# Decay levels of a recurrent mixer: VectorE multiplies only the halves that change, ScalarE copies the rest

## The reference: what is computed

```
f = lb + (1 - lb) * sigmoid(f_logit);  log_f = log(f);  k = 1 - f;  q = silu(q) * scale
b = cumsum(log_f) over the tokens
a[t, s] = sum_k q[t, k] * k[s, k] * exp(b[t, k] - b[s, k])     for s <= t
o = a @ v   (and a state that carries the same decay from chunk to chunk)
```

## Time and profile before

| | |
|---|---|
| median of three executions | 1296.33 us |
| the profiled execution | 1297.8 us, its span 1296.0 us |
| TensorE busy | 1253.4 us (97%) |
| VectorE busy | 993.6 us (77%) |
| ScalarE busy | 617.4 us (48%) |
| recurrent heads at work | from 157 to 386 us of the span |
| mean granted TensorE clock | 0.986 of full speed |

### The profile page before, as it was taken

How to read it: one execution, slowest core, us unless ns; L and a number is a source line. 1 busy time by engine, 2 the same in 40 slices (tenths; PEclk the granted TensorE clock), 3 DMA queues, 4 the chain that set the end, 5 groups by cost and what they waited for, 6 DMA issues and landing times.

```text
span 1296.0 us, 20738 instructions
## 1 busy us (share of the span) xinstructions
PE 1253.4 (97%) x7190; PEld 1105.4 (85%) x7190; DVE 993.6 (77%) x1290; ACT 617.4 (48%) x875; POOL 50.3 (4%) x98
## 2 busy tenths in 40 slices
PE   5899899999999999999999999999999999999997
PEld 5788899998988888888888888888888888888886
DVE  4788799999898889688888797879777766545454
ACT  3335455555556644555444444444444444434342
POOL 0000100031130000000000000000000000000000
PEclk9789899999999999999999999999999999999999
DMA  9999788888798899758777777776666676555553
GB/s 338 387 386 350 274 292 282 275 285 292 244 314 284 296 355 355 263 178 292 243 225 232 241 230 239 238 245 212 191 184 192 194 260 213 194 194 194 195 195 114
DMA packets 155988, 329.44 MB, mean 254 GB/s; under 512 B 11493, under 2 KB 20438, under 8 KB 155026
## 3 DMA queue, kind: packets, MB, share of 16 engines
q1 hardware_dynamic: 152352, 318.49, 74.0%
q0 software_dynamic: 3280, 9.66, 2.2%
q10 hardware_dynamic: 290, 0.44, 0.1%
HBM read 322.77 MB, written 4.19 MB: 252 GB/s over the span
## 4 chain that ended last, share of the span: by engine, by line
PE 86%; DVE 5%; DMA 4%; ACT 2%; issue 2%; SPq 0%; DVEq 0%; ACTq 0%
PE bank L1281 23%; PE bank L1289 12%; PE bank L1346 6%; PE bank L1344 6%; PE bank L1345 6%; PE bank L1026 5%; PE bank L1028 5%; PE bank L1027 5%; PE bank L1013 4%; PE bank L1015 4%; PE bank L1016 4%; DMA pc<-in_w_ada 3%; DVE acc_c L1440 2%; DVE wlo L1428 1%; ACT whi L680 1%
## 5 line engine op out<-in xcount | busy, mean ns | idle before, releaser
L680 ACT ACTIVATE whi<-wraw 128x1024 fp32r<-128x1024 f32 x408 | 425.1, 1059 | 577.5 <-PE bank L1289 229.4
L1428 DVE TENSOR_TENSOR wlo<-wraw,whi 128x1024 fp32r<-128x1024 f32 x404 | 491.4, 1222 | 243.9 <-ACT whi L680 242.6
L1281 PE MATMUL bank<-h,whi 128*128 128x512 f32 x1400 | 334.7, 391 | 1.2 <-DVE h L1694 0.8
L1281 PEld LDWEIGHTS bank<-h,whi 128*128 128x128 f32 x1400 | 257.1, 188 | 51.8 <-issue 1.2
L1289 PEld LDWEIGHTS bank<-h,wlo 128*128 128x128 f32 x1400 | 179.6, 191 | 6.9
L1289 PE MATMUL bank<-h,wlo 128*128 128x256 f32 x1400 | 181.7, 283 | 0.0
L1013 PE MATMUL bank<-h,whi 128*128 128x256 f32 x512 | 149.0, 291 | 4.4 <-DVE h L1453 4.4
L1015 PE MATMUL bank<-h,whi 128*128 128x256 f32 x512 | 146.1, 285 | 0.0
L1016 PE MATMUL bank<-h,wlo 128*128 128x256 f32 x512 | 146.0, 285 | 0.0
L1344 PE MATMUL bank<-whi,act_hi 128*128 128x512 f32 x336 | 130.9, 389 | 0.0
L1346 PE MATMUL bank<-whi,act_lo 128*128 128x512 f32 x336 | 130.7, 389 | 0.0
(11 more groups left out here) (247 smaller groups left out, 1323.9 us busy)
## 6 DMA issues: line engine op xcount, KB each, us to landing
wraw<-in_w_up SPq DMA_DIRECT2D x176, 512.0 KB, 3.8
araw<-in_w_ada SPq DMA_DIRECT2D x128, 512.0 KB, 5.3
wraw<-in_w_in SPq DMA_DIRECT2D x112, 512.0 KB, 4.9
wraw<-in_w_down SPq DMA_DIRECT2D x88, 512.0 KB, 4.1
pc<-in_w_ada SPq DMA_DIRECT2D x48, 512.0 KB, 11.5
wraw<-in_w_out SPq DMA_DIRECT2D x32, 512.0 KB, 6.6
pc<-in_w_ada SPq DMA_DIRECT2D x32, 256.0 KB, 7.0
x<-in_x SPq DMA_DIRECT2D x2, 1024.0 KB, 8.3
```

The lines of the kernel that those rows point to most:

```text
L680: act.activation(whi[:, slot], wraw[:, slot], ACT.Copy).then_inc(s_hi, 1)
L1281: pe.matmul(ps[bank0 + f], whi[:, (ph.unit0 + j) % RING, k, f * P:(f + 1) * P], h[:, kk].rearrange("p a t -> p (a t)"), start=(kk == 0), s ...
L1428: dve.tensor_tensor(wlo[:, slot], wraw[:, slot], whi[:, slot].bitcast(F32), ALU.subtract).then_inc(s_lo, 1)
```

## The change

Three things. The factors are no longer kept per head with 1.0 between them: ScalarE writes f in place into `proj` for four heads ahead of time (steps `DECAY_AT`: 22, 22, 23, 23 and 51 to 54), and VectorE forms the factors of all levels for four heads at once in `decay_tree` (six dependent products of 512, 256, ... 16 elements, at steps 24 and 56). A level is now one VectorE product over the 256 elements that change, and one ScalarE copy (`keep`) of the 256 that don't. And there is one level a step, s0 to s0+5, with the merged keys one step behind each; everything later moves one step: `scores_b` to s0+8, the second `collect` to s0+9, the small `amat` copies to s0+10, `hgrn_out` to s0+11, the squares to s0+12. `ATT_AT` and the steps of the attention part are as before.

```diff
+DECAY_AT = [HGRN_AT[0] - 2 + hd // 2 if hd < 4 else HGRN_AT[4] - 9 + hd for hd in range(HEADS)]
+TREE_AT = [HGRN_AT[0], HGRN_AT[4]]
...
-            gp.memset(tot[:], 1.0).then_inc(s_cst, 1)
...
+            def keep(hd, l):
+
+                if l == 0:
+                    act.wait_ge(s_ks, hd + 1)
+                    act.wait_ge(s_qs, hd + 1)
+                else:
+                    act.wait_ge(s_lv, (LEVELS - 2) * hd + l)
+                    act.wait_ge(s_kept, (LEVELS - 2) * hd + l)
+                act.activation(kept(l + 1, l), kept(l, l), ACT.Copy).then_inc(s_kept, 1)
...
-                    if s == s0 - 1:
+                    if s == DECAY_AT[hd]:
                         act.wait_ge(s_ev, ev(GROUP["hf", hd // 4]))
-                        if hd:
-                            act.wait_ge(s_lv, (LEVELS - 2) * (hd - 1) + 2)
-                        else:
-                            act.wait_ge(s_lb, 1)
-                        sig = proj[:, HF + hd, :]
-                        act.activation(decays(0), sig.rearrange("p (b n c) -> p b n c", b=TB, c=2), ACT.Identity,
+                        act.wait_ge(s_lb, 1)
+                        act.activation(proj[:, HF + hd, :], proj[:, HF + hd, :], ACT.Identity,
                                        bias=lb[:, hd:hd + 1], scale=one_lb[:, hd:hd + 1]).then_inc(s_tot, 1)
...
-                    elif s == s0 + 2:
-                        merge_keys(hd, range(2))
-                    elif s == s0 + 4:
-                        merge_keys(hd, range(2, LEVELS - 1))
-                    elif s == s0 + 9:
+                    if s0 <= s < s0 + LEVELS - 2:
+                        l = s - s0
+                        keep(hd, l)
+                        if l:
+                            merge_keys(hd, l - 1)
+                    elif s == s0 + LEVELS - 2:
+                        merge_keys(hd, LEVELS - 3)
+                        last_level(hd)
+                        merge_keys(hd, LEVELS - 2)
+                    elif s == s0 + 10:
...
-                    elif s == s0 + 11:
+                    elif s == s0 + 12:
...
-                    elif s == HGRN_AT[hd] + 7:
+                    elif s == HGRN_AT[hd] + 8:
                         scores_b(hd)
-                    elif s == HGRN_AT[hd] + 10:
+                    elif s == HGRN_AT[hd] + 11:
                         hgrn_out(hd)
...
+            def decay_tree(g):
+
+                dve.wait_ge(s_tot, 4 * g + 4)
+                if g:
+                    dve.wait_ge(s_last, 3 * 4 * g)
+                for l in range(LEVELS - 2):
+                    a = decays_of_group(l, g)
+                    st.do(dve.tensor_tensor(decays_of_group(l + 1, g), a[:, :, ::2], a[:, :, 1::2], ALU.mult))
+                    st.wait()
+
             def level(hd, l):
-                w, n = 1 << l, P >> l
-                if l < LEVELS - 2:
-                    first, second = (factors_by_block(l)[:, :, e:e + n:2].rearrange("p b (n c) -> p b n c", c=2) for e in (1, n))
...
+                w = 1 << l
+                if l:
+                    dve.wait_ge(s_lv, (LEVELS - 2) * hd + l)
+                    dve.wait_ge(s_kept, (LEVELS - 2) * hd + l)
+                else:
+                    dve.wait_ge(s_ks, hd + 1)
+                factor = decays(l, hd).rearrange("p (n c) -> p c n", c=2).unsqueeze(3).to_broadcast([P, 2, P // w, w])
+                dve.tensor_tensor(changed(l + 1, l), changed(l, l), factor, ALU.mult).then_inc(s_lv, 1)
...
-                    if s == HGRN_AT[hd] + 8:
+                    if s == HGRN_AT[hd] + 9:
                         collect(hd, 1)
...
-                    elif s in (HGRN_AT[hd] + 1, HGRN_AT[hd] + 2, HGRN_AT[hd] + 3):
-                        l = 2 * (s - HGRN_AT[hd])
-                        level(hd, l - 1)
-                        if l < LEVELS - 2:
-                            level(hd, l)
-                    elif s == HGRN_AT[hd] + 5:
+                    elif HGRN_AT[hd] < s < HGRN_AT[hd] + LEVELS - 2:
+                        level(hd, s - HGRN_AT[hd])
+                    if s == HGRN_AT[hd] + 5:
                         collect(hd, 0)
+                for g in range(2):
+                    if s == TREE_AT[g]:
+                        decay_tree(g)
```

More of the change, by code:

```diff
@@ L433, in ev, with decays_of_group, decays, changed @@
             return 2 * n + 2
[L435 to L451, removed]
+        first_of = [0, 0]
+        for l in range(1, LEVELS - 1):
+            first_of.append(first_of[-1] + 4 * TB * (P >> l))
+        def decays_of_group(l, g):
+            if l == 0:
+                return proj[:, HF + 4 * g:HF + 4 * g + 4, :]
+            return tot[:, first_of[l]:first_of[l + 1]].rearrange("p (e x) -> p e x", e=4)
+        def decays(l, hd):
+            return decays_of_group(l, hd // 4)[:, hd % 4, :]
+        def changed(level, of):
+            w = 1 << of
+            base = qk[:, level, 0, w:w + 1]
+            return bass.AP(base.tensor, base.offset, [list(base.ap[0]), [2 * P - w, 2], [2 * w, P // w], [1, w]])
+        def kept(level, of):
+            w = 1 << of
+            base = qk[:, level, 0, 0:1]
+            return bass.AP(base.tensor, base.offset, [list(base.ap[0]), [2 * P + w, 2], [2 * w, P // w], [1, w]])
         def q_of(level, b):
-            return qk[:, level, b, b]
+            return qk[:, level, 3 * b]
         def k_of(level, b):
-            return qk[:, level, b, 1 - b]
+            return qk[:, level, 2 - b]
         def of_both(level, first, second):
@@ L757, in last_level, with merge_keys @@
                     act.activation(new[:, b, 0:w], old[:, b, 0:w], ACT.Copy,
[L758 to L768, removed]
-                    else:
-                        act.activation(k0[:].rearrange("p (n c w) -> p n c w", c=2, w=1), of_both(0, k_of(0, 0), k_of(0, 1)),
-                                       ACT.Copy).then_inc(s_km, 1)
+                                   scale=decays(LEVELS - 2, hd)[:, 2 * b + 1:2 * b + 2]).then_inc(s_last, 1)
+            def merge_keys(hd, l):
+                if l == LEVELS - 2:
+                    act.wait_ge(s_last, 3 * hd + 1)
+                else:
+                    act.wait_ge(s_lv, (LEVELS - 2) * hd + l + 1)
+                    act.wait_ge(s_kept, (LEVELS - 2) * hd + l + 1)
+                if l:
+                    act.activation(second_halves(k_of(l, 0), l), second_halves(k_of(l, 1), l), ACT.Copy).then_inc(s_km, 1)
+                else:
+                    act.activation(k0[:].rearrange("p (n c w) -> p n c w", c=2, w=1), of_both(0, k_of(0, 0), k_of(0, 1)),
+                                   ACT.Copy).then_inc(s_km, 1)
             for s in range(LATER - AHEAD, UP0):
@@ L1515, in second_norm @@
                                              op0=ALU.add, op1=ALU.mult).then_inc(s_colr, 1)
-            def level(hd, l):
-                w, n = 1 << l, P >> l
-                if l < LEVELS - 2:
-                    first, second = (factors_by_block(l)[:, :, e:e + n:2].rearrange("p b (n c) -> p b n c", c=2) for e in (1, n))
[L1521 to L1529, removed]
-                    dve.wait_ge(s_lv, (LEVELS - 2) * hd + l + 1)
-                    st.wait()
+            def decay_tree(g):
[6 more added lines that the diff above has]
+                    st.wait()
+            def level(hd, l):
+                w = 1 << l
+                if l:
+                    dve.wait_ge(s_lv, (LEVELS - 2) * hd + l)
+                    dve.wait_ge(s_kept, (LEVELS - 2) * hd + l)
+                else:
+                    dve.wait_ge(s_ks, hd + 1)
+                factor = decays(l, hd).rearrange("p (n c) -> p c n", c=2).unsqueeze(3).to_broadcast([P, 2, P // w, w])
+                dve.tensor_tensor(changed(l + 1, l), changed(l, l), factor, ALU.mult).then_inc(s_lv, 1)
             def first_level(hd):
-                queries = qk[:, 0].rearrange("p b a (n c) -> p (b a) n c", c=2)[:, ::3]
                 dve.wait_ge(s_ev, ev(GROUP["hq", hd // 4]))
```

31 lines of the change are left out of this document (18 added, 13 removed).

## The result

The changed kernel takes 1303.05 us (median of six, 1300.72 to 1304.86) against 1297.08 us (six, 1295.85 to 1298.98): ratio 1.0045, 95% interval 1.0035 to 1.0055. It is slower by 6.0 us; I had forecast slower by 4.0. The median lies 0.15 us inside the upper bound of my range (1303.2) and above the band of the forecast alone (1299.2 to 1301.6).

A forecast was written before the change was run, and what follows sets the result against it. TensorE was taken as the bound, its pauses in time deciding. Terms 1.0 - 1.0 + 2.66 - 0.24 + 1.57 = +4.0 us on the median of 1296.33 gave 1300.3 us, range 1297.2 to 1303.2.

The forecast's parts named there:

- TensorE's order decides: While the recurrent heads run, only TensorE's pauses count; VectorE's saved work is idle time unless a pause goes with it.
- Term c: Behind unit 90, TensorE waits before attention head 2's scores for ScalarE's small copies, now in step 90: +2.66 us.
- Term d: Behind the new pause at unit 90 the granted clock falls to half: +1.57 us, between 0 and 3.
- the small pause: The pause before `hgrn_out(7)`, now behind unit 91, goes: -0.24 us.
- The rival that the clock holds: The clock stays full behind unit 90: +2.4 us, 1298.8 us in all; chance 0.22.
- The row behind the 1.80 us pause: Earlier profile, before `scores_a` of head 0: half clock and a unit of 4.45 instead of 2.88 us, costing 1.57 us.
- Term b: The pause at 332 us, before attention head 0's transposes, goes because VectorE's reciprocal comes earlier: -1.0 us.
- the rival of late hand-overs: ScalarE late at step s0+11, between `hgrn_out` and the next `scores_a`: 0.5 us for seven heads, 1303.8 us; chance 0.15.
- my signs of being wrong: A pause under 2 us before the third attention head, or pauses before `scores_a` of heads 1 to 7.
- Term a: `scores_a(0)` waits for the second merged key in ScalarE's step 26, which comes later: +1.0 us, between 0 and +2.0.
- the clock is lost before and after alike: 0: At `scores_a(0)` the clock falls in both kernels, so it adds 0 us.
- The tree: VectorE's factor products: 3.1 us if strided, level 1 then 0.2 us late for ScalarE; 2.2 us and in time if plain.

The follow-up runs named there:

- e6: Changed kernel with one more VectorE product of 256 elements in each of the 48 levels, into a tile nothing reads: 1303.73 us, ratio 1.0059 to the kernel before.
- e1: Changed kernel with attention heads 2 and 3 one unit later (scores behind units 91 and 92): 1298.46 us, ratio 1.0014 to the kernel before.
- e3: Changed kernel with the first scores of recurrent head 0 alone behind unit 28 instead of 27: 1297.56 us, ratio 1.0003 to the kernel before.
- e2: Kernel before with only attention head 2's scores moved, behind unit 89 instead of 90: 1304.07 us, ratio 1.0051 to the kernel before.
- e9: Changed kernel with eleven small products of ones ahead of the wait behind unit 90: 1304.50 us, ratio 1.0056 to the kernel before.
- e12: Changed kernel with the two sines and their table load in ScalarE's step 28 instead of 26: 1301.32 us, ratio 1.0028 to the kernel before.
- e8: Kernel before with the first scores of recurrent head 0 alone behind unit 28 instead of 27: 1296.12 us, ratio 0.9993 to the kernel before.
- e10: Kernel before with first scores of recurrent head 0 behind unit 28 and attention head 0 one step later: 1299.99 us, ratio 1.0018 to the kernel before.

## Why the prediction was right, and where it was not

- **That TensorE's order decides and VectorE's relief is worth next to nothing: right.** e6 puts the work back for about 1 us; e1 and e3 change no work at all and move the time by 4.0 and 4.9.
- **Term c, the new pause: right.** 2.66 forecast, 2.66 measured in the changed kernel and the same idle time (2.50) in e2 and, unmended, in e3.
- **Term d, the clock: right in size.** 1.57 forecast; 1.6 by unit 91 (4.54 against 2.96 in the kernel before and 2.94 in e9). c and d with the small pause are 4.0 in the forecast and 4.0 by e1. The rival that the clock holds is out. The row behind the 1.80 us pause was a lucky guide all the same: idle stretches of 1.80, 2.50 and 2.78 us were followed by half clock, those of 0.83, 1.21, 1.47 and 1.78 us were not. 1.78 and 1.80 fall on different sides, so how long a stretch must be isn't shown, nor that its length alone decides.
  The Trainium skill's page "TensorE: Matmul & The Clock Gate" (section "Why this matters for your kernels") warns only of longer gaps, and that is not borne out here.
- **Term b, the pause at 332 us: wrong, 0 instead of -1.0.** The pause of the earlier trace rows did go, but one of the same length came at `hgrn_out(5)`, one unit earlier. The step that failed is "it can normalize by 330" with nothing late in its place: I followed VectorE's gain to the softmax, but not the softmax into ScalarE's step 73, where the table load and the exponentials take 2.2 us (325.46 to 327.65) and make the small copies late, which the change has just moved to step 74. I had put that price in the rival of late hand-overs (0.5 us for each of seven heads); it was one head and 1.0 us. So one of my signs of being wrong, a pause ahead of `scores_a` of a later head, was there once.
- **Term a, the first scores: right in kind, too small.** 1.0 forecast; +2.3 and +3.0 measured, like with like. Two steps of it failed. The first is ScalarE's start of step 24, "some 0.2 us later": the writes of f take 0.50 us each from start to start, not 0.3, so that four of them less the old one are 1.0 us. ScalarE in the changed kernel (first fence) and in e2 (second):

```profile
160.13 1.09 ACT L810 ACTIVATE proj<-proj,small 128x256 f32<-128x256 f32 x2
161.12 1.05 ACT L690 ACTIVATE whi<-wraw 128x1024 fp32r<-128x1024 f32 x1
...
169.03 0.25 ACT L789 ACTIVATE qk<-qk 128x64 f32<-128x64 f32 x1
```
```profile
160.10 1.10 ACT L680 ACTIVATE whi<-wraw 128x1024 fp32r<-128x1024 f32 x1
...
167.53 0.25 ACT L768 ACTIVATE qk<-qk 128x64 f32<-128x64 f32 x1
```

  From there to the second merged key it is 7.91 us, within 0.1 of what I had worked out. The scores start 1.5 us later between the late profiles (169.38 against 167.88) and 1.9 between the early ones (mean 167.7 against 165.77). The second step that failed is "the clock is lost before and after alike: 0". It holds between the early profiles. But in e2, which is the kernel before at this place, TensorE reached it 3.1 us later than in the kernel before's profile, idled 0.83 us, and the clock stayed at 1.00 behind it:

```profile
167.88 0.68 PE L1042 MATMUL bank<-proj,qk 128*128 128x128 f32 x4 [0.83 <-issue]
```
```profile
170.00:172.00 2.00, 2.00 (x20) 2.00 (x19) 1.97 (x4) 0.00 (x0) 0.00 (x0) 1.00 0.87 238
```

  Unit 28 took 2.96 us there, against 4.45 in the changed kernel: 1.5 us more. The changed kernel lost the clock at this place in seven profiles of seven that have it unmended, early or late.
- **The tree: cheaper than I took it.** 128 elements over every second value took 0.292 us, not the 0.401 of the earlier trace rows. It stays a near second at the first scores all the same (e12).
  The Trainium skill's page "SBUF — State Buffer" (section "Door 1: The DMA port swizzle", its note on cachelines) puts no penalty on a stride of two fp32 values, and the 0.292 us, the price that I had estimated for a plain product (0.29), agrees.
- **Small pauses** ahead of `hgrn_out` went for three heads (1, 4 and 7), not for one: 0.9 us (0.3, 0.3 and 0.24) instead of 0.24.

Added up by the marks: like with like 2.3 + 3.1 - 0.2 = 5.2 us between early profiles and 3.0 + 3.1 - 0.2 = 5.9 between late ones, against 6.0 by the medians. Against the forecast of 4.0, term b and term a each missed by 1 us or more in the dear direction and the small pauses by 0.7 in the other. The sum stayed in the range because terms c and d, two thirds of the loss, were right; that it stayed there by 0.15 us was luck. What fills the difference between the marks and the medians is open; there are only a few profiles.

## What to carry to other kernels

Where an order is written by hand and one engine is the bound, count what each moved step is waited for by, above all by work that stays in place: one line of the schedule that was not moved along cost two thirds of the loss here (4.0 of 6.0 us). A pause can have a second price behind it in the clock, and one profile may show a place in its dear or in its cheap case; look at the same place in several, and compare executions that reached it at the same time. Marks for such a comparison must lie behind all that was moved. Relieving an engine that isn't the bound gains only what pauses it caused, and e1 and e3 show that moving one wait by one unit (4.0 and 4.9 us) was worth more than all the arithmetic saved (about 1 us).

## What the runs showed of the hardware

- Sixteen products of one column, 1.7 us of TensorE busy by the profile, were followed in two profiles (e8, e10) by a granted clock of half, 1.2 of 2.4 GHz, and 1.6 us lost; in the other twelve the clock stayed at full. A busy TensorE isn't always enough to keep the clock.
- Behind idle stretches of TensorE of 1.80 us (the kernel before), 2.50 us (the changed kernel, e2) and 2.78 us (e10) the granted clock was half; behind 0.83 and 1.78 us (e2), 1.21 us (the kernel before) and 1.47 us (e9, with eleven small products behind it) it stayed at full. At half clock a product of 512 columns starts 0.43 us behind the one before, at full clock 0.23.
- A ScalarE copy of 256 fp32 elements in SBUF takes 0.418 us, as much as VectorE's product of the same size (0.417), so that halving a product of 512 (0.686 us) between the two engines costs 0.835 us of engine time.
